# Narrow products of a decoder step moved into four column groups: the samples' attention values, and the overflow rows of the two large expert turns

## The reference

```python
D_MODEL = 1024; SEQ = 256; DEC_BATCH = 8; DEC_SEQ = 8; N_MEM = 256
H_C = 4; DH_C = 128; N_EXPERTS = 8; TOP_K = 2; D_FF_E = 2816

# attention into the memory, in each layer; a sample has keys and values of its own
qh = q.reshape(bsz, t, H_C, DH_C)
s = jnp.einsum('bthd,bmhd->bhtm', qh, mem_k) * (DH_C ** -0.5)
p = jax.nn.softmax(s, axis=-1)
o = jnp.einsum('bhtm,bmhd->bthd', p, mem_v).reshape(bsz, t, D_C)
y_c = o @ w_c_out

def swiglu(x, w_g, w_u, w_d):
    return (jax.nn.silu(x @ w_g) * (x @ w_u)) @ w_d

# experts: gates holds a token's two shares, zero elsewhere
for e in range(N_EXPERTS):
    out = out + gates[..., e:e + 1] * swiglu(x, w_gate[e], w_up[e], w_down[e])
```

## Time and profile before

| | |
|---|---|
| median of the runs | 1988.23 us (1987.68 to 1988.99) |
| profiled execution | 1984.89 us, span of the core 1983.1 us |
| busy in the span | PE 1878.6 (95%), PEld 1604.9 (81%), DVE 1482.1 (75%), ACT 1066.3 (54%), POOL 136.5 (7%) |
| layer 0, 1: value stage | 152.1 to 207.0, 769.2 to 822.7 us |
| first and last turn (large) | 1017.9 to 1183.7, 1785.6 to 1951.1 us |
| a small turn | 100.0 us (1685.6 to 1785.6) |
| bytes from HBM | 435.68 MB, 226 GB/s over the span |

### The profile page before, as it was taken

How to read it: one execution, slowest core, us unless ns; L and a number is a source line. 1 busy time by engine, 2 the same in 40 slices (tenths; PEclk the granted TensorE clock), 3 DMA queues, 4 the chain that set the end, 5 groups by cost and what they waited for, 6 DMA issues and landing times.

```text
span 1983.1 us, 28034 instructions
## 1 busy us (share of the span) xinstructions
PE 1878.6 (95%) x10353; PEld 1604.9 (81%) x10354; DVE 1482.1 (75%) x2119; ACT 1066.3 (54%) x1206; POOL 136.5 (7%) x159
## 2 busy tenths in 40 slices
PE   7999999899998999999889999999999999999993
PEld 7899899799987989899766678888888888886672
DVE  6997686755536999667576668888888888886665
ACT  4452754543324444474444456767777776765442
POOL 1110000000001020000020001020202020201000
PEclk9999999899999999999989999999999999999997
DMA  7553344344443563444456569898989898996522
GB/s 268 203 215 143 138 151 144 109 168 149 149 141 116 191 229 136 149 149 150 149 211 250 199 233 339 335 382 331 374 331 380 337 375 333 366 346 241 210 106 87
DMA packets 118613, 446.91 MB, mean 225 GB/s; under 512 B 10384, under 2 KB 10384, under 8 KB 118016
## 3 DMA queue, kind: packets, MB, share of 16 engines
q1 hardware_dynamic: 112288, 424.45, 58.1%
q0 software_dynamic: 6240, 21.33, 3.2%
HBM read 435.68 MB, written 12.67 MB: 226 GB/s over the span
## 4 chain that ended last, share of the span: by engine, by line
PE 42%; issue 3%; DVE 3%; ACT 1%; DMA 1%; SPq 0%; DVEq 0%; POOLq 0%; POOL 0%; ACTq 0%
PE psum L1996 11%; PE psum L1997 11%; PE psum L1998 11%; PE psum L2003 3%; PE psum L2002 3%; ACT wph L616 1%; PE psum L1736 1%; PE psum L2059 1%; DVE wpl L622 1%; DVE hT L1674 0%; DMA x<-out_acc 0%; DMA out_acc<-arena,rows_out 0%; DVE arena L1663 0%; PE psum L2062 0%; DVE x L1164 0%
## 5 line engine op out<-in xcount | busy, mean ns | idle before, releaser
L622 DVE TENSOR_TENSOR wpl<-e_ring,wph 128x2048 fp32r<-128x2048 f32 x269 | 606.9, 2289 | 85.5 <-ACT wph L616 84.5
L616 ACT CAST wph<-e_ring 128x2048 fp32r<-128x2048 f32 x269 | 501.7, 1903 | 119.6 <-PE psum L1998 66.7
L574 DVE TENSOR_TENSOR wl<-ring,wh 128x1024 fp32r<-128x1024 f32 x234 | 285.3, 1223 | 208.1 <-ACT wh L568 207.4
L1750 PE MATMUL psum<-xTh,wh 128*128 128x320 f32 x1184 | 375.3, 317 | 31.6 <-DVE xTl L1266 11.0
L1751 PE MATMUL psum<-xTl,wh 128*128 128x320 f32 x1184 | 369.9, 312 | 0.0
L1752 PE MATMUL psum<-xTh,wl 128*128 128x320 f32 x1184 | 369.7, 312 | 0.0
L568 ACT CAST wh<-ring 128x1024 fp32r<-128x1024 f32 x234 | 243.9, 1046 | 138.6 <-PE psum L1771 71.2
L1996 PE MATMUL psum<-wph,xe 128*128 128x512 f32 (+1 forms) x768 | 293.6, 382 | 2.8 <-issue 2.4
L1997 PE MATMUL psum<-wph,xe 128*128 128x512 f32 (+1 forms) x768 | 289.1, 376 | 0.0
L1998 PE MATMUL psum<-wpl,xe 128*128 128x512 f32 (+1 forms) x768 | 288.7, 376 | 0.0
L1750 PEld LDWEIGHTS psum<-xTh,wh 128*128 128x128 f32 x1184 | 225.7, 191 | 40.0 <-DVE wl L574 15.7
(11 more groups left out here) (327 smaller groups left out, 2528.5 us busy)
## 6 DMA issues: line engine op xcount, KB each, us to landing
e_ring<-experts SPq DMA_DIRECT2D x264, 1024.0 KB, 6.4
ring<-stream SPq DMA_DIRECT2D x274, 512.0 KB, 3.2
lnp<-rows POOLq DMA_DIRECT2D x4, 1024.0 KB, 6.1
x<-x POOLq DMA_DIRECT2D x3, 512.0 KB, 5.8
arena<-x0T SPq DMA_DIRECT2D x2, 640.0 KB, 5.9
o_a<-arena POOLq DMA_DIRECT2D x2, 540.0 KB, 7.6
o_k<-arena POOLq DMA_DIRECT2D x2, 512.0 KB, 7.0
o_v<-arena POOLq DMA_DIRECT2D x2, 512.0 KB, 8.8
```

Source lines behind the costliest of these rows:

```text
L574: dve.tensor_tensor(wl[:, q % SPLITS, :], ring[:, u % SLOTS, :], wh[:, q % SPLITS, :].bitcast(F32), ALU.subtract).then_inc(lo_done, 1)
L616: act.copy(wph[:, SLOT_OF[m % NPOS], :], ring_place(m).rearrange("p u c -> p (u c)")).then_inc(hi_e, 1)
L622: dve.tensor_tensor(wpl[:, s, :], ring_place(m).rearrange("p u c -> p (u c)"), wph[:, s, :].bitcast(F32), ALU.subtract).then_inc(lo_e, 1)
L1750: pe.matmul(out, h[:, k], hi[:, k], start=(k == 0), stop=False)
```

## The change

The values of the samples: the probabilities become stationary (32 columns: a sample's 4 heads x 8 tokens) and the values move, 512 columns. Four samples run in the four column groups of one bank (`ob`). ScalarE copies the bank out (`obs`), four transposes (`ot`) turn it back, and the diagonal blocks (a head's rows against the same head's columns) are the output. The order by hand is `ATTEND`: `ob` 0, two gate blocks, `ot` 0, two blocks, `ob` 1, one block, the mean, one block, `ot` 1, two blocks, the variance. The units of four samples thus stand in the ring before the gate units (`stands_at` keeps their place in memory). Convolution B runs after blocks 0, 1, 2 and 6. ScalarE copies the prompt's part of the output ahead of the gates.

The large turns: tile B's rows are kept as F32 only (`xe_b`, `hT_b`) and multiplied exactly against the raw weights, 32 columns stationary in four column groups. For gate and up, group g takes block g of the chunk (128 columns moving), so a chunk's result is one 128 x 128 block, and one transpose turns it; for down, group g takes a quarter of the model's columns (256 moving). The adding of halves goes, and so do `up_chunk` on ScalarE, `turn_done`, `ys_sum`, `hb_ready` and `hb_sum`. The second scatter writes 128 rows of 256 columns instead of 32 of 1024, so `choose` lists tile B's rows four times, once in each group. As TensorE now reads the raw weights, SP in large turns waits for it (`mm_e`) instead of the split (`lo_e`), the ring starts with six loads instead of ten, and the splits of a large turn come two positions later (`LATER`), the last two at its end.

```diff
+ATTEND = [("ob", 0), ("g", 2, 0), ("g", 2, 1), ("ot", 0), ("g", 2, 2), ("g", 2, 3), ("ob", 1), ("g", 2, 4),
+          ("mean", 0), ("g", 2, 5), ("ot", 1), ("g", 2, 6), ("g", 2, 7), ("var", 0)]
+MEAN_AFTER = 4
...
-SPLIT_AHEAD, LOAD_AHEAD = 5, 10
+SPLIT_AHEAD, LOAD_AHEAD, LATER = 5, 10, 2
...
+FIRST_LOADS = [m for m in range(LOAD_AHEAD) if SLOT_OF[m] not in SLOT_OF[:m]]
+TURN_LOADS = sorted((m for m in range(2 * NPOS) if 0 <= before_in_slot(m) < NPOS and SLOT_OF[m % NPOS] in SLOT_OF[:m]),
+                    key=before_in_slot)
...
+            def expert(i, e, loads, big):
+                for m in loads:
+                    if big:
+                        sp.wait_ge(mm_e, i * NPOS + (before_in_slot(m) + 1))
+                    else:
+                        sp.wait_ge(lo_e, i * NPOS + (before_in_slot(m) + 1))
                     load(m, e + 1 if m >= NPOS else e)
...
-                pool.wait_ge(turn_done, i + 1)
...
+                pool.indirect_dma_start(out_acc.rearrange("t (g c) -> (t g) c", g=GROUPS),
+                                        bass.IndirectOffsetOnAxis(ap=rows_out[:, 1:2], axis=0), ys_b, None,
...
-                for n in range(KT):
-                    gates_of(2, n, None)
                 for n in range(H_C):
                     made(l, "o", n)
-                    act.copy(oTh[:, n], bank(l, "o", n)[:, 0:T]).then_inc(oh_ready, 1)
+                    act.copy(oTh[:, n, 0:SEQ], bank(l, "o", n)[:, 0:SEQ]).then_inc(oh_ready, 1)
+                for key in ATTEND:
+                    if key[0] == "ob":
+                        made(l, *key)
+                        frees(act.copy(obs[:, key[1]], bank(l, *key)), l, *key)
+                    elif key[0] == "ot":
+                        made(l, *key)
+                        act.copy(four_samples(oTh, key[1]), diagonal(bank(l, *key))).then_inc(oh_ready, 1)
+                    elif key[0] == "g":
+                        gates_of(2, key[2], None)
...
-                        act.copy(gate_b[0:CAP_B, 0:w], psum[CAP_B:2 * CAP_B, BANK_X, 0:w])
+                        act.activation(sg_b[0:rows], psum[0:rows, BANK_X, 0:P], ACT.Sigmoid)
...
-                    expert_hi(act, n + SPLIT_AHEAD, i)
+                    if not big:
+                        expert_hi(act, n + SPLIT_AHEAD, i)
+                    elif n >= LATER:
+                        expert_hi(act, n + SPLIT_AHEAD - LATER, i)
...
+                for m in range(NPOS + SPLIT_AHEAD - LATER, NPOS + SPLIT_AHEAD) if big else ():
+                    expert_hi(act, m, i)
...
-                    for c in range(2):
-                        act.copy(ys_b[0:CAP_B, 512 * c:512 * c + 512], psum[CAP_B:2 * CAP_B, BANK_DB + c, :])
+                    act.activation(ys_b, psum[:, BANK_DB, 0:D_OF], ACT.Copy, scale=gate_out[:, 1:2])
...
-                    if n in (0, 1, 5, 6):
-                        conv_b({0: 0, 1: 2, 5: 4, 6: 6}[n])
+                    if n == 3:
+                        samples_lo(0)
+                    if n in (0, 1, 2, 6):
+                        conv_b({0: 0, 1: 2, 2: 4, 6: 6}[n])
...
-                        dve.wait_ge(hb_ready, i * NJ + (j + 1))
-                        dve.tensor_tensor(gate_b[0:CAP_B, 0:w], gate_b[0:CAP_B, 0:w], sg_b[0:CAP_B, 0:w], ALU.mult)
...
+                        dve.tensor_tensor(h_b[0:rows, 0:P], psum[0:rows, BANK_T, 0:P], sg_b[0:rows], ALU.mult)
+                        dve.tensor_tensor(h_e[:, 0:w], psum[:, BANK_U, 0:w], sg_e[:, 0:w], ALU.mult)\
                            .then_inc(hid_done, 1)
...
+                def attend(q):
+                    four = range(4 * q, 4 * q + 4)
+                    w = [weights(pe, l, "cv", b).rearrange("p (m c) -> p m c", m=2) for b in four]
+                    take(pe, l, "ob", q)
+                    for m in range(2):
+                        for n, b in enumerate(four):
+                            c = 2 * P * m + 32 * b
+                            ins = product(bank(l, "ob", q)[32 * n:32 * n + 32, :], pT[:, H_C, c:c + 32], w[n][:, m], m, 2)
...
+                    for g in range(GROUPS):
+                        ins = product(chosen[CAP_B * g:CAP_B * g + CAP_B, 3:6], pick[:, t, P:CAP], values[:, t, :],
+                                      t, 3)
...
+                def into_b(kind, j, b):
+                    weight = [ring_place(AT[kind, f])[:, u] for f in CHUNKS[j] for u in range(2)]
                     for k in range(KT):
+                        for g, w in enumerate(weight):
+                            ins = pe.matmul(psum[CAP_B * g:CAP_B * g + CAP_B, b, 0:P], xe_b[:, k],
+                                            w[:, P * k:P * k + P], start=(k == 0), stop=(k == KT - 1),
+                                            skip_group_check=True)
+                    ins.then_inc(mm_e, len(CHUNKS[j]))
...
-                            if big:
-                                ins = packed(BANK_DB + c, slice(0, 512), th[:, BOTH_B], th[:, HI_B], h[:, u, cs],
-                                             low[:, u, cs], False, final)
+                        for g in range(GROUPS if big else 0):
+                            ins = pe.matmul(psum[CAP_B * g:CAP_B * g + CAP_B, BANK_DB, 0:D_OF],
+                                            th_b,
+                                            ring_place(AT["down", f])[:, u, D_OF * g:D_OF * g + D_OF],
+                                            start=False, stop=final, skip_group_check=True)
```

More of the change, by code:

```diff
@@ L1151, in _ @@
         def _(dve):
-            for _ in range(24):
+            for _ in range(20):
                 dve.sem_inc(dve_placed, 1)
@@ L1877, in attend @@
                     step(ins)
-                for br, yk in BRANCHES:
-                    for n in range(KT):
-                        if br == 2:
-                            attend(n)
-                        blocks((l, "g", br, n), xTh, xTl, T)
-                        if (br, n) == (2, MEAN_AFTER):
-                            pe.wait_ge(conv_a_tap, K_A * (l + 1))
-                            take(pe, l, "mean", 0)
-                            for j in range(JA):
-                                ins = product(bank(l, "mean", 0)[:, 0:T], ones[:], ca[:, j], j, JA)
-                            step(ins)
-                    if br == 2:
+                for key in ATTEND:
+                    if key[0] == "ob":
+                        attend(key[1])
+                    elif key[0] == "ot":
+                        samples_turned(key[1])
+                    elif key[0] == "g":
+                        blocks((l, *key), xTh, xTl, T)
+                    elif key[0] == "mean":
+                        pe.wait_ge(conv_a_tap, K_A * (l + 1))
+                        take(pe, l, "mean", 0)
+                        for j in range(JA):
+                            ins = product(bank(l, "mean", 0)[:, 0:T], ones[:], ca[:, j], j, JA)
+                        step(ins)
+                    else:
@@ L1896, in _ @@
                         step(ins)
+                for br, yk in BRANCHES:
+                    for n in range(KT if br != 2 else 0):
+                        blocks((l, "g", br, n), xTh, xTl, T)
                     if br == 1:
@@ L1904, in _ @@
                             emptied(pe, l, "o", h)
+                        for q in range(2):
+                            emptied(pe, l, "ot", q)
                     else:
@@ L1958, in choose @@
                 for t in range(3):
-                    ins = product(chosen[0:CAP_B, 3:6], pick[:, t, P:CAP], values[:, t, :], t, 3)
+                    for g in range(GROUPS):
+                        ins = product(chosen[CAP_B * g:CAP_B * g + CAP_B, 3:6], pick[:, t, P:CAP], values[:, t, :],
+                                      t, 3)
                 ins.then_inc(idx_mm, 1)
```

221 lines of the change are left out of this document (100 added, 121 removed).

## The result

The changed kernel takes **1944.4 us** (median of four runs, 1943.1 to 1945.6) against 1988.6 before on the same chip: ratio 0.9776, interval 0.9759 to 0.9793. The forecast was 1932, range 1908 to 1955. The profiled execution of after took 1945.6 (span 1943.7), 1.2 above its median; that of before (1984.9, span 1983.1) lay 3.7 under the 1988.6. So the spans of the two traces stand 39.4 us apart where the medians stand 44.2 apart.

A forecast was written before the change was run, and what follows sets the result against it. TensorE bounds the large turns and the value stage, there with VectorE close behind. Large turns -45.3, small turns +1.2, end -2.2 and value stage -10 sum to -56: 1929 for the profiled execution, 1932 us for the median, range 1908 to 1955.

The forecast's parts named there:

- The price of a set: Large turns: a chunk's narrow gate or up product in four column groups takes 2.06 us instead of 3.71.
- a down half: Large turns: a down product's narrow records in four groups take 0.74 us instead of 0.94, 22 times, -4.4 a turn.
- the list: List of rows, every turn: 18 added records cost between 0 and 0.9 us; 0.2 taken, +1.2 for six small turns.
- the 0.4 for position 5: Start of a large turn: position 5's weights, loaded when gate 0 ends, come late for gate 1, +0.4 us.
- (a): Rival, large turns: changes of width cost nothing, 20 us less, 1912; chance 0.13.
- (b): Rival, large turns: issue of the small records is the limit, a set costs 3.5 us, 1967; chance 0.10.
- (e): Rival: the four groups don't run together at 128 columns, a set costs 7.3 us, 2125; chance 0.03.
- (d): Rival, sample values: the attention stage gives nothing, 1942; chance 0.05.
- (c): Rival, large turns: loads land 6 us later, each of ten chunks waits 3 us, 1962; chance 0.07.
- two turns -45.3: First and last of eight turns: each large turn saves 22.7 us on TensorE, together 45.3.
- Value stage, layer 0: Sample values, layer 0: VectorE's splits decide, -7.1 us, less 1.7 for the low clock, leaving -5.4.
- The end: End of last turn: shorter scaling and way to GpSimd, -0.7 - 2.1, +0.6 for the second scatter: -2.2 us.

The follow-up runs named there:

- attn_alone: The kernel before with the sample-value stage alone changed: 1973.5 us against 1991.1 in its comparison, ratio 0.9915.
- late_acc: After, with the 1.28 MB that GpSimd writes from x to the sum held back until the first turn's seventh split is done: 1941.4 us, ratio 0.9772.
- best_c: After, with GpSimd's writes of x held back, the down products' narrow halves together and the first turn's sixth load behind the router's inputs: 1930.8 us, ratio 0.9707.
- moe_alone: The kernel before with all of the change except the value stage, the turns alone: 1958.5 us, ratio 0.984.
- pad_before: The kernel before with 548 never-executed instructions between the large and the small turn's code of TensorE: 1988.1 us, ratio 0.9997.
- unrolled_before: The kernel before with a large turn's four double chunks written out in TensorE's program instead of looped, same products in the same order: 1995.5 us, ratio 1.0035.
- down_once: After, with the narrow down products of both halves of a position together behind its twelve wide ones: 1938.3 us, ratio 0.9752.

## Why the prediction was right, and where its steps were off

**What carried it.** The price of a set (2.06, measured 2.08) and of a down half (0.74 and 0.77) came from one block of the same form in the earlier trace rows, and both stood. So did that of the list, which was a choice between 0 and 0.9 (+0.2 and +0.24: 1787.07 to 1788.25 against 0.94 in the earlier trace rows). The last large turn is 24.0 shorter instead of 22.7; the transposes gave most of the difference (0.46 a chunk against 0.89 to 0.95 in the trace of before, nearly twice the gain that the prediction took), and the 0.4 for position 5 was not lost there. Rivals (a), (b) and (e) fall with these rows, (d) with attn_alone, whose trace is 11.3 us shorter. (c), late loads, happened in one place, the first turn's 2.40 us, not in every chunk; 6.6 us lie between the two large turns of after, of which late_acc takes 4.9 away.

**Where luck came in.** The gain is 44 us of the 56 forecast. The time lies in the range because that was kept wide for rivals that did not come true, and it is near the 1942 of rival (d) for another reason than (d)'s. Most of the missing 12 us went where no rival had looked; (c) names a part of it.

**The step that failed** is "two turns -45.3": what was worked out for the last turn was doubled, and the passage between the first and the second turn was taken as it stood. The prediction counted TensorE's instructions as durations and not as code. The stop cost 7.6 us, and the second turn, with the clock at 0.50 from 1164.1 to 1174.3, took 2.5 more. In the first turn, position 5 was given +0.4 with a landing of 4.8 us; it cost a wait of 2.40 and the low clock behind it, with landings of 7.1 to 9.0. Against late loads the prediction held a DMA share of 0.45, which is the last turn's; the first turn's was 0.64 in before already. The stop's 7.6, the second turn's 2.5 and the 5.3 missing in the first turn are 15.4 of the 16.6 us between the forecast for the profiled execution (1929) and what it took (1945.6).

**Mis-sized terms.** Value stage, layer 0: -5.4, as forecast, with both stalls on VectorE's split weights where they were put (3.3 and 2.1 us instead of 3 and 3) and the low clock behind the first. That the figure is met to the tenth is luck: in seven of the eight other traces with the same stage it takes 51.0 to 52.1 us and not 49.6. In late_acc, say, with stalls of 3.4 and 1.9, the clock falls to 0.50 behind the second one too (181.2 to 184.6); its row in the table by stretches:

```profile
151.20:202.30 51.10, 44.39 (x265) 38.91 (x265) 43.70 (x108) 19.74 (x30) 0.00 (x0) 0.93 0.49 180
```

Against before's 54.9 the usual gain in layer 0 is thus some 4 us, as in layer 1. Layer 1: -2.3 instead of -4.6. Some of that is the trace of before, which kept the full clock there (1.00 in its row above); in the three other traces of this stage unchanged (moe_alone, pad_before, unrolled_before) it takes 55.0 to 55.9 us, not 53.5, and against these the gain is 3.8 to 4.7. Branch C was to follow as before, but is 1.5 and 1.7 shorter; in layer 0 a wait of 1.0 us for the last convolution is gone, which now comes earlier on VectorE. The router lost 3.4: 1.6 of it is the sixth load ahead of its inputs, which best_c gets back, and 1.4 the idle time at the first turn's first product, for which the row names no releaser and which stays in best_c. The list was given +0.2 for every small turn; the five behind the second together lost 0.2.

**The end** gained 0.9 instead of 2.2. The timeline of after's last turn (all engines), the answer to the earlier trace rows:

```profile
1908.71 5.50 ACT L639 CAST wph<-e_ring 128x2048 fp32r<-128x2048 f32 x3
...
1912.10 0.64 PE L2088 MATMUL psum<-e_ring,hT_b 128*32 128x256 f32 x8
1914.12 0.47 ACT L1168 ACTIVATE arena<-psum,gate_out 128x256 f32<-128x256 f32 x1
1914.48 1.26 ACT L1170 ACTIVATE arena<-psum,gate_out 128x512 f32<-128x512 f32 x2
...
1916.79 2.05 POOL L870 DMA_INDIRECT out_acc<-arena,rows_out  x1 [120.22 <-issue]
...
1919.14 1.57 POOL L873 DMA_INDIRECT out_acc<-arena,rows_out  x1 [0.30 <-issue]
```

These are the roundings of ScalarE, the last products, the scaling and the two scatters. The splits that come two positions later end up at the turn's end: three roundings keep ScalarE until 1914.1, 1.4 us past the last product, and the scaling queues behind them. The prediction moved the splits and did not look at what stands behind them on ScalarE there. The scatter begins 4.1 us after the last product (TensorE ends at 1912.7), not 3.

## What to carry to other kernels

Price a new form of product from a block of the same form that is already in the trace, changes of width included: sets and down halves held to 4% here, and putting the narrow products of two halves together then won a third of a microsecond each time. Count instructions as code too: where a loop with two kinds of body stops being held, a passage between them can cost a bare jump (here the first one, 10.0 us; the passage into the last large turn cost none), and the row to read is the sequencer's branch with its longest duration, together with the instruction queue. And price each round of a loop by its own surroundings: the first one shares the DMA queues and its clock with what went before.

## What the runs showed of the hardware

- A long jump, read as one to code that is not held, took 3.3 to 5.0 us in these runs (3.4 at the end of after's last turn, 4.99 in before); as the second of two beside a burst of loads 5.8 to 7.4, with the loads held back 4.9. The others took 0.07 to 0.26, their median 0.2.
- Four column groups cost no more than two: a set of 64 records takes 1.88 us, one of 32 in two groups 1.87.
- Loads of 1 MB that landed after 4.8 to 6.9 us with 1.28 MB of writes held back (late_acc) took 7.1 to 9.0 beside them (after).
- Going into four column groups and out again cost 0.34 us a pair (down_once: 3.75 us for eleven pairs).
